# Modulation 2 weighted on DVE in attention's output stage and summed at the second routing; modulation 3 spread over every second chunk of the first MLP

## What is computed

```python
def ada_mod(c, w, b):
    m = (jax.nn.silu(c) @ w + b)[:, None, :]
    shift, scale, gate = jnp.split(m, 3, axis=-1)
    return shift, scale, 1.0 + gate
...
for layer in range(DEPTH):
    shift, scale, gate = ada_mod(c, ada_w[layer, 0], ada_b[layer, 0])
    u = x * (1.0 + scale) + shift
    ...
    x = layer_norm(ALPHA * x + gate * y, ln_g[layer, 0], ln_b[layer, 0])
    shift, scale, gate = ada_mod(c, ada_w[layer, 1], ada_b[layer, 1])
    u = x * (1.0 + scale) + shift
    y = jnp.square(jax.nn.relu(u @ mlp_w1[layer] + mlp_b1[layer])) @ mlp_w2[layer] + mlp_b2[layer]
    x = layer_norm(ALPHA * x + gate * y, ln_g[layer, 1], ln_b[layer, 1])
```

## Time and profile before

| what | value |
|---|---|
| median of 3 runs | 2884.91 us (2884.13 to 2894.32) |
| profiled execution | 2893.18 us, of which its span 2891.4 us |
| PE busy | 2566.1 us, 89% |
| DVE busy | 1874.9 us, 65% |
| ACT busy | 1366.2 us, 47% |
| mean granted clock of PE | 0.927 |

### The profile page before, as it was taken

One profiled execution on the slowest core, in us unless ns is written; L12 is line 12 of the kernel. 1 busy time (PEld: TensorE's weight loads), 2 busy tenths in 40 slices (PEclk: granted clock), 3 DMA queues, 4 the chain that ended last, 5 costly groups with the idle time before them and its releaser, 6 DMA issues.

```text
span 2891.4 us, 31119 instructions
## 1 busy us (share of the span) xinstructions
PE 2566.1 (89%) x11522; PEld 2033.9 (70%) x11522; DVE 1874.9 (65%) x2237; ACT 1366.2 (47%) x1901; POOL 211.8 (7%) x221
## 2 busy tenths in 40 slices
PE   5879999778996999997987889989798998899997
PEld 2668888566775888884665667778666666688886
DVE  4679999644635999985863756545774664644356
ACT  2258888533633888884522322123332563332321
POOL 1022222100001222211000000000000000000000
PEclk9789999888997999998996889999998899899999
DMA  7379991431013999615220245443211002222230
GB/s 259 112 300 365 367 361 69 174 115 46 16 44 131 369 365 367 251 63 212 73 73 29 80 165 199 149 142 116 74 60 44 1 1 102 80 102 102 73 110 29
DMA packets 100374, 418.57 MB, mean 145 GB/s; under 512 B 25737, under 2 KB 26081, under 8 KB 60785
## 3 DMA queue, kind: packets, MB, share of 16 engines
q1 hardware_dynamic: 70976, 373.27, 35.5%
q0 software_dynamic: 29248, 43.32, 4.2%
HBM read 484.91 MB, written 48.76 MB: 185 GB/s over the span
## 4 chain that ended last, share of the span: by engine, by line
PE 74%; DVE 15%; ACT 5%; issue 3%; DMA 2%; POOL 0%; SPq 0%; DVEq 0%; ACTq 0%; POOLq 0%
PE psum L107 22%; PE psum L108 21%; PE psum L109 21%; PE psum L742 2%; DVE w_low L260 2%; ACT w_high L246 1%; PE psum L1532 1%; DVE ada_sum L1564 1%; PE psum L486 1%; PE psum L357 1%; DVE rg_in L2181 1%; DMA raw<-in_ada 1%; DVE gla_head L2181 1%; PE psum L759 1%; DMA rows<-in_rows 1%
## 5 line engine op out<-in xcount | busy, mean ns | idle before, releaser
L260 DVE TENSOR_TENSOR w_low<-raw,w_high 128x2048 fp32r<-128x2048 f32 (+1 forms) x216 | 485.3, 2258 | 260.2 <-ACT w_high L246 247.9
L246 ACT ACTIVATE w_high<-raw 128x2048 fp32r<-128x2048 f32 (+1 forms) x216 | 405.7, 1886 | 317.6 <-PE psum L109 304.2
L107 PE MATMUL psum<-x_high,w_high 128*128 128x512 f32 x848 | 348.4, 411 | 39.6 <-DVE w_low L260 25.3
L108 PE MATMUL psum<-x_high,w_low 128*128 128x512 f32 x848 | 339.6, 400 | 0.0
L109 PE MATMUL psum<-x_low,w_high 128*128 128x512 f32 x848 | 337.8, 398 | 0.0
L107 PE MATMUL psum<-w_high,mlp_high 128*128 128x512 f32 x512 | 205.1, 401 | 27.5 <-DVE mlp_low L932 11.5
L107 PEld LDWEIGHTS psum<-x_high,w_high 128*128 128x128 f32 x848 | 160.6, 189 | 87.2 <-issue 40.4
L109 PE MATMUL psum<-w_low,mlp_high 128*128 128x512 f32 x512 | 205.3, 401 | 0.0
L108 PE MATMUL psum<-w_high,mlp_low 128*128 128x512 f32 x512 | 204.9, 400 | 0.0
L107 PE MATMUL psum<-w_high,xg_high 128*128 128x512 f32 x480 | 195.7, 408 | 6.2 <-DVE xg_low L853 6.2
L108 PEld LDWEIGHTS psum<-x_high,w_low 128*128 128x128 f32 x848 | 160.5, 189 | 43.7 <-issue 6.4
(11 more groups left out here) (542 smaller groups left out, 5410.4 us busy)
## 6 DMA issues: line engine op xcount, KB each, us to landing
raw<-in_moe SPq DMA_DIRECT2D x138, 1024.0 KB
raw_extra<-in_moe SPq DMA_DIRECT2D x102, 1024.0 KB
raw<-in_mlp SPq DMA_DIRECT2D x64, 1024.0 KB
raw<-in_ada SPq DMA_DIRECT2D x48, 1024.0 KB
rows<-in_rows POOLq DMA_DIRECT2D x20, 512.0 KB, 4.7
raw<-in_evin SPq DMA_DIRECT2D x10, 1024.0 KB
raw<-in_foxqk SPq DMA_DIRECT2D x8, 1024.0 KB
xn_rows<-xn_tiles POOLq DMA_DIRECT2D x9, 512.0 KB, 3.0
```

Source lines behind the costliest of these rows:

```text
L107: pe.matmul(out, ah, bh, start=first, stop=False)
L108: pe.matmul(out, al, bh, start=False, stop=False)
L246: act.activation(k.WH[k.W_AT[c]][:, 0:w], k.RAW[k.RAW_AT[c]][:, 0:w], ACT.Copy).then_inc(*k.A.step("high", c))
L260: dve.tensor_tensor(wl[:, 0:w], k.RAW[k.RAW_AT[c]][:, 0:w], wh[:, 0:w].bitcast(F32), ALU.subtract).then_inc(*k.V.step("low", c))
```

## The change

- `load_list`: the 12 pieces of modulation 2 are loaded behind attout's last chunk wo3, in one row, ahead of moe 1's first chunk. The 12 of modulation 3 are loaded behind chunks 3, 5, ... 25 of mlp 1.
- `attout_vector`: DVE does piece 0 behind wo1's split, piece 1 and wo2's split, piece 2 and wo3's split, pieces 3 to 5, the four additions of half 0, pieces 6 to 9, the four additions of half 1.
- `route_vector` of route 1: pieces 10 and 11 ahead of the wait for the logits; `ada_done(2)` behind the split of moe 1's first chunk.
- `route_tensor` of route 1: the six groups of sums of modulation 2 behind the last logits, into bank 7.
- `ada_total`: modulation 2 gets six accumulators of its own (`ACC6`, one a pair), so its pieces wait for no sums. Modulation 3 keeps the one buffer and its wait.
- `mlp_pieces`: in mlp 1 one piece behind chunks 3, 5, ... 25, modulation 3 alone; `ada_done(2)` and the wait for it leave the stage.

```diff
--- before.py
+++ after.py
@@ -167,9 +167,9 @@
     follow = {0: [(0, n) for n in range(ADA_PARTS)]}
     for n in range(ADA_PARTS):
         follow.setdefault(k.MOE0[n // 6] + 3 * NBLK - 1, []).append((1, n))
-    m = k.FIRST[("mlp", 1)]
-    for n in range(2 * ADA_PARTS):
-        follow.setdefault(m + 3 + n - (n + 1) // 6, []).append((2 + n // ADA_PARTS, n % ADA_PARTS))
+    for n in range(ADA_PARTS):
+        follow.setdefault(k.FIRST[("attout",)] + 3, []).append((2, n))
+        follow.setdefault(k.FIRST[("mlp", 1)] + 3 + 2 * n, []).append((3, n))
     out = []
     for c in range(len(k.CH)):
         out.append(c)
@@ -500,6 +500,9 @@
     if L == 0:
         pe.wait_ge(*k.after("ada picked", 0, 3))
         ada_rows(k, pe, 0, 5, 7, (10,))
+    else:
+        for n in range(ADA_PARTS):
+            ada_sums(k, pe, 2, n, 7)
     pe.wait_ge(*k.after("picked", L))
     pe.wait_ge(*k.after("count", L))
     pe.matmul(k.PS[:, 5, 0:(T + 1) * NE], const(k, "upper"), k.PICK[:, 0:T + 1, :], start=True, stop=False)
@@ -561,6 +564,9 @@
     dve.tensor_copy(k.IDS[:, 0:2 * T, :].rearrange("p a c -> p (a c)"), k.AID[:, 0:4 * T]).then_inc(*V.step())
     dve.wait_ge(*V.now())
     dve.tensor_scalar(k.IDS[:, 0:2 * T, :], k.IDS[:, 0:2 * T, :], 1.0, None, ALU.add).then_inc(*V.step())
+    if L:
+        ada_piece(k, dve, 2, ADA_PARTS - 2)
+        ada_piece(k, dve, 2, ADA_PARTS - 1)
     dve.wait_ge(*k.after(name, "logits", T - 1))
     lg = k.LG[:, 0:T, :]
     at, _ = _R["rbias"]
@@ -602,6 +608,8 @@
         *V.step("picked", L))
 
     split_low(k, dve, c0)
+    if L:
+        ada_done(k, dve, 2)
     dve.wait_ge(*k.after("ranked", L))
     cnt, nb, end = k.CNT[:, 0, :], k.CNT[:, 1, :], k.CNT[:, 2, :]
     dve.tensor_copy(cnt, k.PS[:, 5, T * NE:(T + 1) * NE]).then_inc(*V.step())
@@ -1487,8 +1495,16 @@
 
 
 def attout_vector(k, dve):
-    split_low(k, dve, k.FIRST[("attout",)] + 3)
+    c = k.FIRST[("attout",)]
+    split_low(k, dve, c + 1)
+    for n in range(6):
+        ada_piece(k, dve, 2, n)
+        if n in (1, 2):
+            split_low(k, dve, c + n + 1)
     for half in range(2):
+        if half:
+            for n in range(6, ADA_PARTS - 2):
+                ada_piece(k, dve, 2, n)
         for t in range(XT):
             dve.wait_ge(*k.after("att rows", half, t))
             cols = slice(half * HALF, half * HALF + HALF)
@@ -1548,16 +1564,21 @@
             *k.V.step("ada picked", s, g))
 
 
+def ada_total(k, s, n):
+
+    return k.ACC[:, :] if s == 3 else k.ACC6[:, n // 2, :]
+
+
 def ada_piece(k, dve, s, n):
 
     w = k.RAW[k.RAW_AT[(s, n)]]
-    acc = k.ACC[:, :]
+    acc = ada_total(k, s, n)
     dve.wait_ge(*k.after("raw", (s, n)))
     for i in range(4):
         f = 4 * (n % 2) + i
         if f == 0:
-            if s > 2 or n:
-                dve.wait_ge(*k.after("ada sums", *((s, n - 1) if n else (s - 1, ADA_PARTS - 1))))
+            if s == 3 and n:
+                dve.wait_ge(*k.after("ada sums", s, n - 1))
             dve.tensor_scalar(acc, w[:, 0:ADA_COLS], k.CS[:, 0:1], None, ALU.mult).then_inc(*k.V.step())
         else:
             dve.wait_ge(*k.V.now())
@@ -1572,11 +1593,9 @@
     if n % 2 == 0:
         return
     pe.wait_ge(*k.after("ada piece", s, n))
-    if s == 3 and n == 1:
-        pe.wait_ge(*k.after("modulation", 2))
     for i in range(4):
-        at = 24 * (s % 2) + 4 * (n // 2) + i
-        mm = pe.matmul(k.PS[:, bank, at:at + 1], k.ACC[:, i * P:(i + 1) * P], const(k, "ones")[:, 0:1], start=True, stop=True)
+        at = 4 * (n // 2) + i
+        mm = pe.matmul(k.PS[:, bank, at:at + 1], ada_total(k, s, n)[:, i * P:(i + 1) * P], const(k, "ones")[:, 0:1], start=True, stop=True)
     mm.then_inc(*k.T.step("ada sums", s, n))
 
 
@@ -1588,10 +1607,8 @@
         dve.wait_ge(*k.V.now())
         src = k.MODC[:, s, :]
     else:
-        bank = 3
-        ps = 24 * (s % 2)
         dve.wait_ge(*k.after("ada sums", s, ADA_PARTS - 1))
-        src = k.PS[:, bank, ps:ps + 3 * DK]
+        src = k.PS[:, 7 if s == 2 else 3, 0:3 * DK]
         dve.tensor_copy(k.MODC[:, s, 2 * DK:3 * DK], src[:, 2 * DK:3 * DK]).then_inc(*k.V.step())
     dve.tensor_tensor(k.MODC[:, s, 0:DK], src[:, 0:DK], k.PARAM[:, at:at + DK], ALU.add).then_inc(*k.V.step())
     dve.scalar_tensor_tensor(out=k.MODC[:, s, DK:2 * DK], in0=src[:, DK:2 * DK], scalar=1.0,
@@ -2473,7 +2490,7 @@
 
 def mlp_pieces(n):
 
-    return [(2 + a // ADA_PARTS, a % ADA_PARTS) for a in range(2 * ADA_PARTS) if 3 + a - (a + 1) // 6 == n]
+    return [(3, a) for a in range(ADA_PARTS) if 3 + 2 * a == n]
 
 
 def mlp_sums(k, pe, s, n):
@@ -2543,8 +2560,6 @@
                                          op0=ALU.mult, op1=ALU.add).then_inc(*k.V.step("partial", s, m))
         if f4 == QT - 1:
             break
-        if s == 1 and f4 == 1:
-            ada_done(k, dve, 2)
         for half in range(2):
             cols = slice(half * HALF, half * HALF + HALF)
             if half:
@@ -3185,6 +3200,7 @@
     k.BE = k.at("route_be", [P, OVER], k.end)
     assert k.end <= picked
     k.SQR1 = k.at("route_squares_late", [P, D], k.XLAT)
+    k.ACC6 = k.at("ada_sums", [P, ADA_PARTS // 2, ADA_COLS], k.end)
 
     k.keep = top - 1024
     k.GATE = k.at("gate", [P, 2, XT + 1], k.keep)
```

## The result

The changed kernel takes 2864.6 us (median of 13 runs, 2860.7 to 2881.88) against 2885.07 (13 runs, 2880.26 to 2895.83) for the kernel before on the same chip. The ratio is 0.9928 [0.9911, 0.9945]: 20.5 us or 0.7% faster. The prediction was 34.5 us, and 2864.6 lies 1.6 us above its range. The profiled execution took 2863.28 us with a span of 2861.5.

A forecast was written before the change was run, and what follows sets the result against it. The prediction took PE to bound the kernel: 44.0 us won in the first MLP less 9.5 paid in attout and route 1 gives 34.5 less, from 2884.9 to 2850.4 us, with an 8-in-10 range of 2842 to 2863.

The forecast's parts named there:

- the first MLP: First to last ReLU of the first MLP: from 360.6 to 316.6 us, a gain of 44.0 us.
- The three steps: First MLP: six groups of sums stay at 0.81 us each, three short waits total 1.4 us, clock 1.00.
- The rival of short waits that break the clock: First MLP: three short waits each bring a slow patch of 2.6 us, 2858 us in all; chance 0.1.
- The handoff rival: First MLP: DVE and PE still wait for each other at five even pieces, 41.5 us back, 2890.5 us; chance 0.04.
- three loads in a row: Attout: DVE waits for three serial piece loads, 4.7 us each from issue to use; last addition 8.2 us late.
- The squares: ACT, end of attout: first mean square starts when its row block is added; first scaled row 9.2 us late.
- the clock of the second routing: Route 1: PE's pace taken from the earlier logits, 0.11 us a record, the fast clock.
- the prediction's own signs: Route 1: DVE at the logits' wait for under 0.5 us, PE's sums ending before the picks.
- the sums are hidden: Route 1: six groups of sums take 4.9 us at the fast clock, within PE's 6.61 us idle before the picks.
- the slow case: Route 1: at half pace the sums take 9.7 us and the picks wait 3.1 us.
- 0.2 that was charged for what was to be hidden: Route 1: pieces 10 and 11 hidden in DVE's idle time before the logits, 0.2 us lost at most.
- The range's end at 14 us of cost: Attout and route 1: upper cost bound, each load a microsecond later and half of the slow sums' cost.

The follow-up runs named there:

- experiment 8: Kernel after with modulation 3's pieces behind consecutive chunks 3 to 14 of mlp 1 instead of every second one; 0.9984 against the kernel before, median 2883.65 us.
- experiment 3: Kernel after with 54 unused dense matmuls on PE between attout's last product and the second routing's transposes; 0.9920 against the kernel before, median 2863.84 us.
- Experiments 2: Kernel before with 11 dummy DVE additions ahead of half 1's additions in attout, so rows come late; 1.0065 against the kernel before, median 2905.82 us.
- experiments 5: Kernel after with wo2's split ahead of pieces 0 to 2 and wo3's behind piece 2; 0.9854 against the kernel before, median 2846.5 us.
- experiment 6: Kernel after with wo2's split first and pieces laid between additions (first kernel, 2846.81 us); the second also divides the sums between logits and ranks (2849.39 us).
- experiments 4: Kernel after with all six groups of sums behind the ranks' product, ada_done(2) one split later; 0.9897 against the kernel before, median 2859.69 us.
- experiments 1: Kernel after without modulation 2's loads, pieces and sums, modulation 0 read instead; 0.9842 against the kernel before, median 2844.56 us.
- experiment 7: Second kernel of experiment 6 with 15 unused dense matmuls ahead of the first routing (first, 2837.69 us); 8 more at attout's end (second, 2844.56 us).

## Why the prediction was right and wrong

**Right: the first MLP.** 316.6 forecast, 317.0 measured. The three steps hold one by one: the sums of six groups stayed, the waits at the last row block are three (0.3 us each, 0.45 forecast), and the clock is 1.00. The rival of short waits that break the clock falls with the third. The rule of the Trainium skill ("TensorE: Matmul & The Clock Gate", A second HAM failure mode), by which moments of idle time between groups of matmuls cost throughput, did not decide here: three waits of 0.3 us left the granted clock at 1.00 for 317 us. The handoff rival falls too; experiment 8 shows a smaller form of it, 15.6 us in place of 41.5, at half the distance.

**Right in kind, too small: three loads in a row.** First scaled row 9.2 us late forecast, 11.1 measured. Last addition 8.2 forecast, 9.9 measured. The term that was mis-sized is the time from issue to use of a modulation load: 4.7 us taken from one load that ran alone, 5.1, 6.1 and 5.2 measured, 2.4 us more over three. The 0.2 us for the signal in the 4.7 is a guess that no run measures by itself. The squares behaved as forecast: the first starts when its row block is added, at 877.05, and the first scaled row starts 3.05 us later, a table load within it (forecast 884.6 to 887.7, 3.1). PE had no wait for a split of wo1, wo2 or wo3 in attout, as forecast. This step is 1.9 us of the miss.

**Wrong: the clock of the second routing.** The step is the sentence "The clock there is taken from the logits". Its 0.11 us a record came from a routing that PE entered after 2.17 us of idle time. The prediction let PE idle 9.3 us longer and kept the figure. Nothing in it asks at which clock PE runs after that. The measured figure is 0.22 a record, and the transposes take 1.97 us for eight against 1.09 at 1.00 (experiment 3): 8.3 us from the first scaled row to the logits, of which 0.1 was forecast. Experiments 2 and 3 show it from both sides: late rows without the change bring the slow routing, and work in place of the idle time takes it away. One of the prediction's own signs caught it: DVE was to wait for the logits for under 0.5 us, and waited 8.62. The trace of before held a warning. This is the first routing in it, the same code, entered after 3.77 us of idle time; a row of the timeline, then the window behind it:

```profile
103.67 1.09 PE L357 MATMUL psum<-const,xn_tiles 128*128 128x128 f32 x8 [3.77 <-DVE xn_tiles L339]
...
110.00:130.00 20.00, 20.00 (x92) 19.37 (x92) 2.49 (x9) 8.81 (x11) 0.53 (x1) 0.50 0.13 51
```

Its first eight transposes still take 1.09 us, the fast figure; then PE is busy for all 20 us of the window at a clock of 0.50. A routing that stays slow while PE has no gap was visible, and with it the price: half pace in transposes and logits.

**Wrong as a consequence: the sums are hidden.** The prediction worked out the slow case, 9.7 us of sums and a wait of 3.1, and set it aside on the ground of the same clock. Measured 10.4 us and 3.4. Experiments 3, 5 and 6 add that even a fast routing would not have kept its clock through the sums: with it at 1.00 at their start, they still cost 2.4, 2.5 and 1.6 us of lg to ranks. The 0.1 us a record taken from the earlier trace rows was right as long as the clock was 1.00, for the first 7 to 18 records; behind the fall each takes 0.21. The forecast took the clock from the logits and kept it for all 48.

**The sum of the miss.** 1.9 for the loads, 8.2 for the clock and 3.4 for the sums, less 0.2 that was charged for what was to be hidden, make 13.3 us of cost too little (22.8 - 9.5). With 0.4 less won in the MLP that is 13.7, the whole of 34.5 - 20.8. The range's end at 14 us of cost took the loads late and half of the slow sums. It had no term for a slow routing, which was the largest part of the miss.

## What to carry to other kernels

When a change makes TensorE wait longer ahead of a stretch of thin matmuls or transposes, price that stretch at both clock levels, and look for another stretch of the same code in the trace that was entered after a longer wait: here a delay of 11 us grew to 19 by it. Work that is moved onto an idle engine has to be placed by when its buffers come free; the same ten pieces cost 11 us to the next stage or 0.4, by where the splits that free the buffers stand among them. And tiny matmuls in a row are not free filler for TensorE: price them at the low clock too, divide them between two gaps, and check that the wait that they stand in front of is still there afterwards.

## What the runs showed of the hardware

**The clock after an idle time isn't settled by its length.** In the second routing, four profiles with 13.0 to 13.5 us of idle time (the kernel after, experiments 2, 4 and 8) stayed at 0.50 throughout. The eight others, with 0.3 to 5.3 us, kept 1.00 or came back to it before the logits. But the first routing, entered after 3.7 to 4.3 us without matmuls put ahead of it, did either: it ran slowly in the profiles of before and of experiments 1, 2, 5 and 8 (3.7 to 3.8 us of idle time; in before, 2 and 8 its first eight transposes still took the fast 1.09 us), and came back in those of the kernel after, of experiments 3 and 4, and of the first kernel of 6 (all 4.2 to 4.3) and the second of 6 (3.8). The longer idle times are among those that came back. What tells the two apart stays open: that an idle time of 13 us leads to a slow second routing is shown, and why is not. That a stretch in which TensorE is busy throughout can keep the low clock for 20 us is shown.

**The clock falls behind a fast routing, with or without sums.** 48 records of sums in a row took 8.55 to 10.38 us: one starts 0.11 us behind another at 1.00, as in the earlier trace rows, and 0.21 at 0.50. In the six profiles with sums behind a fast routing (experiments 3 and 5, and both kernels of 6 and of 7) the clock fell while they ran, with TensorE's busy share at 100%, 0.7 to 1.9 us behind the last logits. But in the kernel before and in experiment 1, which have no sums there, it fell 1.0 to 1.1 us behind the last logits, with TensorE idle since. Two windows of the kernel before, logits in the first and no work in the second:

```profile
888.00:892.00 4.00, 4.00 (x39) 4.00 (x37) 0.00 (x0) 3.54 (x5) 0.00 (x0) 1.00 0.06 24
...
894.00:898.00 4.00, 0.00 (x0) 0.00 (x0) 3.56 (x14) 0.83 (x2) 0.00 (x0) 0.50 0.00 0
```

So that the sums bring the fall about isn't shown; it may come from the transposes and logits ahead of them, and no experiment separates the two.

**Runs of one kernel lie in groups some 9.5 us apart**, and the profiles show two places where it comes from. One is the first routing: wo1's split starts at 833 to 834 us in the profiles where it ran at 0.50, and at 821 to 825 in those where it came back or ran at 1.00 throughout. This accounts for the two spans: 2891.4 - 2861.5 = 29.9 is 9.5 from the first routing and 20.8 from the change, less 0.4 elsewhere. It does not make the result: seven runs of the kernel before lie at 2880 to 2885 and eight of the kernel after at 2861 to 2865, and the medians of these are 20.4 us apart.

The other is a stretch of the last attention. From the start of the first MLP's last ReLU to the end of the span it is 893.3 to 894.2 us in nine profiles and 902.8 to 904.4 in three (the first kernel of experiment 6, the second of 7, experiment 8). Windows 240 to 480 us behind that ReLU, first the kernel after, then the first kernel of experiment 6:

```profile
2208.10:2448.10 240.00, 216.77 (x990) 163.31 (x989) 133.02 (x309) 120.18 (x321) 0.00 (x0) 0.91 0.11 40
```

```profile
2185.00:2425.00 240.00, 217.50 (x950) 163.34 (x949) 132.21 (x307) 117.37 (x319) 0.00 (x0) 0.86 0.10 36
```

The mean clock over this stretch is 0.91 in all nine profiles of the short kind and 0.86 in all three of the long; the kernels don't differ there. Why it differs stays open. It is why steps under 10 us were read from the timelines here and not from medians of four runs.
